# One float32 encoder layer on one core: a recurrence's two score matrices added before their product, the squares of a norm added up on VectorE, two first weight tiles split one block early, and the query and expert blocks made one

## What is computed

```
hn   = modulate(rmsnorm(x), sh1, sc1);  proj = hn @ w_in            # 28 column tiles of 128
o_h  = hgrn2(q, f_fwd, f_bwd, i, g)     # 4 heads: gated linear recurrence in chunks of 64, both ways
         # within a chunk: scores = tril(qr @ kr^T); o_intra = scores @ v   (forward and backward added)
o_c  = silu(layernorm(depthwise_conv31(a * sigmoid(gate))))
h    = x + g1 * (concat(o_h, o_c) @ w_out)                           # 8 column tiles
hn2  = modulate(rmsnorm(h), sh2, sc2)   # mean of squares over the 1024 columns of h
q    = hn2 @ wq                         # 16 tiles: 8 heads x 2 halves; scores against 128 keys each
top16 x top16 -> top16 of 16384 experts per head and token
h    = h + g2 * sum_j softmax_j * gelu(hn2 . u[e_j]) * v[e_j]
out  = modulate(rmsnorm(h), fsh, fsc)
```

## Time and profile before

| what | value |
|---|---|
| median of 3 runs | 2977.69 us (2970.37 to 2980.58) |
| the profiled execution | 2967.23 us, its span 2965.5 us |
| PE busy | 2812.0 us, 95% |
| DVE busy | 2238.2 us, 75% |
| POOL busy | 1257.6 us, 42% |
| ACT busy | 865.6 us, 29% |
| moved by DMA | 911.43 MB, 307 GB/s over the span |

### The profile page before, as it was taken

How to read it: one execution, slowest core, us unless ns; L and a number is a source line. 1 busy time by engine, 2 the same in 40 slices (tenths; PEclk the granted TensorE clock), 3 DMA queues, 4 the chain that set the end, 5 groups by cost and what they waited for, 6 DMA issues and landing times.

```text
span 2965.5 us, 31534 instructions
## 1 busy us (share of the span) xinstructions
PE 2812.0 (95%) x10212; PEld 1534.2 (52%) x10212; DVE 2238.2 (75%) x4571; ACT 865.6 (29%) x1715; POOL 1257.6 (42%) x1091
## 2 busy tenths in 40 slices
PE   6999899897899999999999999999999999999995
PEld 3677677776745444554454545544444444444442
DVE  5898565316789999998998978876767677667675
ACT  3223464213111113673673766810000000000004
POOL 1001110212355445444444454464666566556551
PEclk9999899998899999999999999999999999999998
DMA  4641111232389999999999999999999999999994
GB/s 202 242 177 43 44 36 58 78 116 89 100 342 377 413 374 373 377 377 382 371 373 379 374 376 410 416 408 396 402 404 404 406 392 399 405 406 396 404 388 184
DMA packets 282607, 911.43 MB, mean 307 GB/s; under 512 B 25808, under 2 KB 73168, under 8 KB 275152
## 3 DMA queue, kind: packets, MB, share of 16 engines
q0 software_dynamic: 147456, 536.94, 46.4%
q1 hardware_dynamic: 97648, 297.56, 26.6%
q10 hardware_dynamic: 37344, 74.98, 6.6%
HBM read 826.01 MB, written 83.36 MB: 307 GB/s over the span
## 4 chain that ended last, share of the span: by engine, by line
DVE 20%; DMA 20%; PE 19%; POOL 8%; issue 4%; DVEq 1%; ACT 1%; SPq 1%; another core or an unknown queue 0%; ACTq 0%; POOLq 0%
DMA s_slot<-in_v,s_row 18%; PE s_pu L1711 15%; DVE s_slot L2127 10%; POOL s_slot L1662 8%; PE s_pw L1748 2%; DVE s_hB L2141 2%; PE s_py L1758 1%; DMA s_wr<-s_w 1%; DMA s_slot<-in_u,s_row 1%; DVEq L2162 1%; DVE pk_key L1372 1%; DVE pk_rep L1373 1%; DVE pk_key L1381 1%; DVE s_eq L2036 1%; SPq L1620 0%
## 5 line engine op out<-in xcount | busy, mean ns | idle before, releaser
L1711 PE MATMUL s_pu<-s_hn,s_ut 128*128 128x512 f32 x2304 | 1012.2, 595 | 4.0 <-issue 3.9
L1662 POOL DMA_INDIRECT s_slot<-in_v,s_row x512 | 627.9, 1226 | 385.1 <-DVE s_hB L2141 269.4
L2141 DVE SCALAR_TENSOR_TENSOR s_hB<-s_slot,s_dot,s_hB 128x1024 f32<-128x1024 f32 x469 | 593.9, 1284 | 250.3 <-DMA s_slot<-in_v,s_row 229.2
L1662 POOL DMA_INDIRECT s_slot<-in_u,s_row x512 | 504.9, 986 | 578.1 <-DVE s_slot L2127 492.4
L1711 PEld LDWEIGHTS s_pu<-s_hn,s_ut 128*128 128x128 f32 x2304 | 434.9, 191 | 531.9 <-issue 531.8
L2127 DVE SCALAR_TENSOR_TENSOR s_slot<-s_slot,s_ph 128x1024 f32<-128x1024 f32 x512 | 607.6, 1219 | 65.8 <-DMA s_slot<-in_u,s_row 40.1
L1893 ACT ACTIVATE s_hotw<-s_hot,s_rest 128x128 bf16<-128x128 bf16 x1024 | 308.7, 424 | 27.3 <-ACT s_gst L1840 20.5
L1950 ACT ACTIVATE s_sq<-y 128x512 f32<-128x512 f32 x16 | 8.9, 627 | 921.1 <-DVE y L2202 921.1
L1792 PE MATMUL s_pw<-s_ct,s_vt 128*128 128x512 f32 x512 | 247.5, 606 | 23.5 <-DMA s_vt<-in_v_tiles 23.5
L335 PE MATMUL s_ps<-hn_hi,w_hi 128*128 128x512 f32 x576 | 236.4, 410 | 20.3 <-POOL w_lo L323 11.8
L1792 PE MATMUL s_pu<-s_ct,s_vt 128*128 128x512 f32 x512 | 243.1, 597 | 0.0
(11 more groups left out here) (306 smaller groups left out, 3001.4 us busy)
## 6 DMA issues: line engine op xcount, KB each, us to landing
s_ut<-in_u_tiles SPq DMA_DIRECT2D x128, 512.0 KB
s_vt<-in_v_tiles SPq DMA_DIRECT2D x32, 2048.0 KB
s_g<-s_gst ACTq DMA_DIRECT2D x120, 256.0 KB
s_w<-s_wb ACTq DMA_DIRECT2D x15, 2048.0 KB
s_wr<-s_w SPq DMA_DIRECT2D x16, 1920.0 KB
s_gr<-s_g SPq DMA_DIRECT2D x60, 512.0 KB, 24.8
s_ada<-in_ada SPq DMA_DIRECT2D x48, 512.0 KB, 6.1
s2w_raw<-in_w_in SPq DMA_DIRECT2D x26, 512.0 KB, 3.9
```

Of the source, the lines that this page charges most:

```text
L1662: pool.indirect_dma_start(out=slot[s][:, :], out_offset=None, in_=io[kind], in_offset=bass.IndirectOffsetOnAxis(ap=row[b][:, j:j + 1], axi ...
L1711: mm = pe.matmul(pu[:, n % 2, :], ut[n % UR][:, k, :], hn[:, k, :], start=(k == 0), stop=(k == DC - 1))
L2141: dve.scalar_tensor_tensor(y, s, dot[b][:, j:j + 1], y, ALU.mult, ALU.add).then_inc(taken, 1)
```

## The change

Five edits, and what they move with them:

1. **Scores added first.** After the second part of the state updates DVE adds `st[0]` and `st[1]` into a new tile `st_both`, and PE makes one product of it with the values in place of two.
2. **First tiles split one block early.** At the end of step1 ACT and POOL make both parts of w_in tile 2 (`m.first`), so that ACT's first instruction in `front` is the sigmoid. In `front` they do the same with w_out tile 2 (`m.second`; SP loads it right behind the tiles of `mix`), for step4.
3. **Squares added by DVE.** In step4 DVE adds the squares of columns 0 to 6 (`add_square`) into `sq_sum`; PE makes only two products with ones, at the end.
4. **step5 goes into step6.** All engines have its code unrolled at the head of the expert block, with no barrier between. DVE's constants come ahead of the picks. POOL's two additions for `hn` come behind the remainders of heads 1 and 2. PE's `turn_h` comes behind the last scores, in the order 1, 0, 3, 2, and ACT's softmax behind the copies of them. SP's first u loads wait for the projections that use the same place.
5. **PSUM is shared**: `pu` and `pw` also serve queries and scores, and `ph` and `py` are the accumulators of the blocks before.

```
@@ step1, ACT and POOL, at the end
+            act.wait_ge(ahead, 32)
+            act.activation(m.first[0][:, :, :], m.front_raw[0][:, :, :], ACT.Copy).then_inc(first_hi, 1)
...
+            pool.wait_ge(first_hi, 1)
+            pool.tensor_tensor(m.first[1][:, :, :], m.front_raw[0][:, :, :], m.first[0][:, :, :].bitcast(F32), ALU.subtract)
@@ front
+            sp.dma_start(next_w[0][:, :, :], io["w_out"][2]).then_inc(second_in, 16)
             sp.wait_ge(o_ready, HEADS)
...
-                mm = project(pe, ps[n % 2], w.hi[n % 2], w.lo[n % 2], m.hn_hi, m.hn_lo, ks)
+                hi, lo = m.first if n == 2 else (w.hi[n % 2], w.lo[n % 2])
+                mm = project(pe, ps[n % 2], hi, lo, m.hn_hi, m.hn_lo, ks)
...
-                    pe.matmul(po[:, c], vtok[:, b, :], st[0][:, b, :], start=True, stop=False)
-                    pe.matmul(po[:, c], vtok[:, b, :], st[1][:, b, :], start=False, stop=False)
+                    pe.matmul(po[:, c], vtok[:, b, :], st_both[:, b, :], start=True, stop=False)
...
-            round_tile(2)
             sigmoid(0)
...
             square_of(3)
+            act.wait_ge(second_in, 16)
+            act.activation(m.second[0][:, :, :], next_w[0][:, :, :], ACT.Copy).then_inc(second_hi, 1)
...
                 for part in range(4):
+                    if part == 2:
+                        dve.tensor_tensor(st_both[:, :, :], st[0][:, :, :], st[1][:, :, :], ALU.add)
@@ step4
-            w.round(act, 1, 0)
             w.round(act, 1, 1)
...
-                if k == 2:
-                    sums(0)
-                sums(k - 1)
-            sums(DC - 1)
+            pe.wait_ge(sq_summed, 1)
+            sums(sq_sum, True, False)
+            pe.wait_ge(sq_ready, DC)
+            sums(sq[:, (DC - 1) % 2, :], False, True)
...
+            def add_square(k):
+                dve.wait_ge(sq_ready, k + 1)
...
             for k in range(DC):
+                if k >= 3:
+                    add_square(k - 2)
...
+            add_square(DC - 2)
+            dve.sem_inc(sq_summed, 1)
             dve.wait_ge(root, 1)
@@ step6, POOL
-            for n in range(2):
-                ks = slice(n * DC // 2, (n + 1) * DC // 2)
...
+            for h in range(1, PH):
+                for s in range(2):
+                    wq.remainder(pool, h, s)
+                if h <= 2:
+                    ks = slice((h - 1) * DC // 2, h * DC // 2)
...
@@ step6, PE
-            turn_h(3, pu[:, :, :].rearrange("p a t -> p (a t)"))
-            turn_h(2, pw[:, :, :].rearrange("p a t -> p (a t)"))
...
+            for h in range(1, PH):
+                for s in range(2):
+                    wq.ready(pe, h, s)
+                    pe.wait_ge(q_ready, h * 2 + s + 1)
+                    project(pe, pu[:, s, :], wq.hi[s], wq.lo[s], m.hn_hi, m.hn_lo, halves=(0,)).then_inc(wq.used, 1)
+                    if s:
+                        scores(h, 0)
+                scores(h, 1)
             turn_h(1, py)
             turn_h(0, ph)
+            pe.wait_ge(q_ready, 2 * PH + 2)
+            turn_h(3, pu[:, :, :].rearrange("p a t -> p (a t)"))
+            pe.wait_ge(sc_taken, 2 * PH + 2)
+            turn_h(2, pw[:, :, :].rearrange("p a t -> p (a t)"))
             pe.wait_ge(h_kept, 3)
```

More of the change, by code:

```diff
@@ L156, in step1 @@
         w_in, w_rounded = [sem(f"s1_w_in{s}") for s in range(2)], sem("s1_w_r")
-        ahead = sem("s1_ahead")
+        ahead, first_hi = sem("s1_ahead"), sem("s1_first_hi")
+        m.first = [at(f"s1_first{i}", [P, DC, P], F32R, F0 + (56 + 4 * i) * KB) for i in range(2)]
         m.front_raw = raw_weights(m, "s2w", R0 + 112 * KB)
@@ L491, in _ @@
                 sp.dma_start(next_x[:, i, :], io["xT"][i]).then_inc(next_in, 16)
-                sp.dma_start(next_w[i][:, :, :], io["w_out"][2 + i]).then_inc(next_in, 16)
-            sp.wait_ge(next_in, 64)
+            sp.dma_start(next_w[1][:, :, :], io["w_out"][3]).then_inc(next_in, 16)
+            sp.wait_ge(next_in, 48)
         @block.gpsimd
         def _(pool):
-            for n in range(2, 4):
-                w.remainder(pool, n // 2, n % 2)
+            w.remainder(pool, 1, 1)
             pool.memset(hd.reset[:, :], 1.0)
@@ L1130, in step4 @@
         ps = m.ps
[L1131 removed]
+        m.pu = m.hold.enter_context(nc.psum_tensor("s4_pu", [P, 2, HALF], F32))
+        ps_q = [m.pu[:, s, :] for s in range(2)]
         ps_ss = ctx.enter_context(nc.psum_tensor("s4_ss", [P, T], F32))
@@ L1173, in _ @@
         def _(pool):
-            for k in range(2, DC + 2):
+            for k in range(3, DC + 2):
                 w.remainder(pool, k // 2, k % 2)
@@ L1178, in _, with sums @@
         def _(pe):
-            def sums(k):
-                pe.wait_ge(sq_ready, k + 1)
+            def sums(src, first, last):
                 for h in range(2):
                     mm = pe.matmul(ps_ss[:, h * HALF:(h + 1) * HALF], m.ones[:, :],
-                                   sq[:, k % 2, h * HALF:(h + 1) * HALF], start=(k == 0), stop=(k == DC - 1))
-                mm.then_inc(sq_used, 1)
+                                   src[:, h * HALF:(h + 1) * HALF], start=first, stop=last)
+            pe.sem_inc(w.rounded, 1)
+            pe.sem_inc(w.split, 1)
             w.begin(pe)
@@ L1759, in add_side, with scores @@
                 mm.then_inc(side_done, 1)
-            turn_h(3, pu[:, :, :].rearrange("p a t -> p (a t)"))
-            turn_h(2, pw[:, :, :].rearrange("p a t -> p (a t)"))
+            def scores(h, s):
+                pe.wait_ge(q_ready, h * 2 + s + 3)
+                pe.wait_ge(sc_taken, h * 2 + s + 1)
+                for b in range(SPARSE):
+                    mm = pe.matmul(pw[:, s, b * P:(b + 1) * P], q[s][:, b * P:(b + 1) * P], m.keysT[:, s, :],
+                                   start=True, stop=True)
+                mm.then_inc(sc_made, 1)
+            wq.begin(pe)
+            pe.sem_inc(q_ready, 2)
+            pe.sem_inc(wq.used, 2)
+            for s in range(2):
+                scores(0, s)
+            for h in range(1, PH):
+                for s in range(2):
+                    wq.ready(pe, h, s)
[4 more added lines that the diff above has]
+                scores(h, 1)
             turn_h(1, py)
             turn_h(0, ph)
+            pe.wait_ge(q_ready, 2 * PH + 2)
+            turn_h(3, pu[:, :, :].rearrange("p a t -> p (a t)"))
+            pe.wait_ge(sc_taken, 2 * PH + 2)
+            turn_h(2, pw[:, :, :].rearrange("p a t -> p (a t)"))
             pe.wait_ge(h_kept, 3)
@@ L2217, in _, with encoder_layer @@
                                              ALU.mult).then_inc(xn_ready[h], 1)
-STEPS = (step1, front, step4, step5, step6)
-def encoder_layer(nc, io, out, steps=5, scratch="Internal"):
+    m.hold.close()
+STEPS = (step1, front, step4, step6)
+def encoder_layer(nc, io, out, steps=4, scratch="Internal"):
     m = Mem()
@@ L2268, in sem @@
             return sems[-1]
-        step(nc, m, io if n < 5 else {**io, "out": out}, sem)
+        step(nc, m, io if n < 4 else {**io, "out": out}, sem)
         nc.clear_and_free_semaphores(sems)
```

165 lines of the change are left out of this document (65 added, 100 removed).

## The result

The changed kernel's median is 2956.9 us in 18 runs, that of the kernel before 2977.4 in 18; the ratio is **0.9939, 95% interval 0.9926 to 0.9952**. (It is not the quotient of the two medians, which are 20.5 us apart.) By the ratio that is 18 us (14 to 22) where 25 were forecast: the sign and the range hold, and the size is 7 us short.

What follows compares the result with a forecast made beforehand. PE, busy 95%, was taken as the bound, with DMA also full in the expert block. Terms -1.6 -1 -2.0 -10.5 +6 -16 = -25.1 gave 2942.1 us, scaled to a median of 2952.5; range 2934 to 2969.

Steps and rivals of the forecast that it cites:

- Start of `front`: Start of `front`: PE's gap falls from 5.6 to 4.0 us, the sigmoid being next to be waited for; -1.6.
- Scores added first: Heads 0 to 3: one PE product fewer per 128 tokens, DVE's addition partly unhidden; -1, bounds -7.4 and +3.7.
- Squares on DVE: Step4: turns of 10.9 us in place of 12.64, -10.5; tail +6, as POOL's subtraction delays DVE's last addition.
- rival (c): End of step4: the tail is cheap, clock and port both kind; 4.3 us less, 2948; chance 0.08.
- Seam, PE: Step5 to step6: PE's barrier idle goes, -10.1; faster `turn_h`, -6.5; u passes, -1.5; ACT's last copy, +1.0; together -17.1.
- Seam, DVE and gathers: Step5 to step6: small casts move ahead and the barrier goes; -10.0 for the ranking and first gather.
- I carry -16: Seam term: PE gains 17, gathers 10, DVE makes up the difference from its waits; bounds -10 and -17.6.
- My own sign of being wrong: Expert block: first u tile to last v product stays 2094 us, give or take 3; a longer way means wrong.
- rival (a): Expert block: the gathers set the end, so it gains 10 in place of 16; 2958.5; chance 0.15.
- rival (b): First gathers: the unexplained stall of 9 to 10 us at a u tile goes; -9 more, 2943.5; chance 0.11.
- Rival (d): Expert block: the gain is spent again, PE's v-tile waits grow; -9 left, 2968.6; chance 0.11.
- Rival (e): First gathers: slower, the stall grows with unrolled code and no barrier; five more such tiles give 2996; chance 0.05.

Runs made afterwards that it cites:

- first pair: First profiled execution of each kernel, unedited: 2967.2 us for the kernel before, 2966.4 us for the changed kernel.
- second pair: Each kernel profiled once more, nothing edited: ratio 0.9942 for the changed kernel, 1.000 for the kernel before.
- before, again and paced: Kernel before: unedited (2977.4 us), unedited once more (ratio 1.000), and with POOL's gathers waiting for PE from tile 92 on (0.9981).
- changed, again and paced: Changed kernel: unedited (ratio 0.9939), unedited once more (0.9942), and with POOL's gathers waiting for PE from tile 92 on (0.9896).
- more rows: Changed kernel with row quota 3.7 instead of 3.5 in tiles 30 to 92, 3.8 instead of 4.3 in 93 to 117: ratio 1.0048.
- the wait on POOL's queue: From tile 92 on, rows of tile n+1 are asked for only after PE finishes tile n-2: changed kernel 0.9896, kernel before 0.9981.
- the later tables: Changed kernel with the first turning of picks and the side rows two tiles later: ratio 0.992; with the wait on POOL's queue too, 0.9891.
- the last experiment's: Changed kernel with the two states not added first (two products on PE again, no addition on DVE): ratio 0.9918.

## Why the prediction was right, and where it was off

- **Start of `front`**: -1.6 forecast. The gap fell from 5.60 to 3.47, -2.1, with the sigmoid as the next late thing, as said: the table load moved up too.
- **Scores added first**: -1 forecast, nothing measured. The gap of 2.3 us was right (2.15). What I left out is that a gap of 2.15 us can bring PE out at the lower level of its clock (3.09 us for 16 products in the first profile, 1.71 in the second); in heads 1 to 3 one of 1.1 did not. It is inside the bounds of -7.4 and +3.7.
- **Start of step4**: -2.0 forecast, -1.5 measured.
- **Squares on DVE**: turns of 10.88, six times 1.76 less: -10.6 against -10.5. The tail: +6 forecast, +1.1 measured (from step4's first product to the first of the queries 91.54 us before, 82.04 after, which is -9.5). The step that failed is "so the addition ends at 669.4": DVE's addition followed its residual without a pause, POOL's subtraction began beside it, and POOL's took longer, not DVE's. And the eight passes ran at the upper level, 3.7 us behind a gap of 2.56. That is rival (c), and below my lower bound of +1.7. The lock of the Trainium skill's page "SBUF — State Buffer", "Who interferes with whom", is in the rows, 3.43 us for 2.35, but on POOL; who comes second is the schedule's to say.
- **Seam, PE**: from the last scores to the first u tile 23.9 us before and 8.2 after, -15.7; forecast -10.1, -6.5 and +1.0, together -15.6. `turn_h` took 7.3 us. **Seam, DVE and gathers**: the first gather came 18.9 us earlier, against 9.1 + 10 by the terms (-1.6 -1 -2.0 -4.5 ahead of the seam).
- **First u tile**: -24.5 in all in the first pair, against -24.7 by my terms. That they agree so closely is luck: step4 began at 586.28 before and 586.29 after, so that nothing was left of the 4.6 us forecast ahead of it, and the cheap tail gave 4.9 back. In the second pair step4 began 4.4 us earlier, and the first u tile came 30.5 us earlier.
- **"I carry -16"** is the step that was off. I took PE's gain and let DVE make up the difference. The runs show the other order: at tile 26 PE waits for what follows from the first gather, and tile 28 keeps its 328 to 333 us from that gather. At tile 28 the change leads by 18 us in the mean (before, again and paced, 1156.2; changed, again and paced, 1137.9), and 18 is what was measured. Delays speak for it too, within wide intervals: gathers 14 us later cost 12, PE 28 us later cost 7. My own sign of being wrong came as well: from the first u tile to the last v product it is 2094.0 us before and 2120.3 after, where I wanted 2094 give or take 3. That is rival (a), the gathers, though by a mechanism with a place in it (the wait at tile 26) that the earlier trace rows couldn't show, as PE did not wait there in the profile of before.
- **How much of the 7 us is this step is open.** In the seam term I carried 6 us more than the gathers gained, but the gathers' gain in all, 19 us, also holds the cheap tail. The jam is the other candidate. With it taken from both kernels by the same wait, the change is worth 0.9896 / 0.9981 = 0.9915, 25 us, with some 7 us to either side, which allows both the forecast and the gathers' 19; the wait gave the changed kernel 13 us and the one before 6. The two were timed on different chips, and their profiled executions are 13 us apart.
- **The stall of the earlier trace rows** (rival b) belongs to both kernels, and its size is chance. From the first u tile of the table to ACT's gelu behind tile 0, 16 tiles on, it is 130.4 us in the first profile of the changed kernel, where the stall is absent, and 131.9 with more rows, but 137.1 to 141.6 in the other eight profiles that have the new seam. So rival (b) did not come true as a rule. What the stall takes from PE lies ahead of the wait at tile 26, and the distance from the first gather to tile 28 is the same with it and without it.
- **Rival (d)**, the gain spent again in the expert block, left 9 us; in the first pair of profiles 0.8 are left, and in the medians 18. PE's waits for v tiles, which it expected to grow, are 22.3 us after and 23.5 before. The first profile of before had no jam, that of the changed kernel had.
- **Rival (e)** has its mechanism in the rows, products one by one while gathers have the DMA engines, but not its trigger, unrolled code: the same stood in the kernel before too.
- **The level**: my scaling from one execution to the median assumed a proportion. Most likely the 10 us were one jam that this execution was spared: tiles 96 to 100 took 15 us less than in the second profile.

Best version: the changed kernel with the wait on POOL's queue, 0.9896, or with the later tables too, 0.9891.

## What to carry to other kernels

In a block where DMA is full, measure a lead also at the first transfer of the queue that feeds it, not only at the first product; here an engine's lead over that was mostly slack, and was lost at the next meeting point. A prefetcher that is limited only by its buffers runs ahead when its consumer is free for a while, and fills the DMA engines just when the critical engine should go on: tie it to that engine's progress. A quota did not do it here, a wait did. And take a second profile of the kernel before ahead of any prediction of under 1%: here one 15 us event made two profiles equal that stand for kernels 18 us apart.

## What the runs showed of the hardware

- **While gathers hold the DMA engines, PE, ACT and SP nearly stop together.** For 25 us the gathers had 102.7% of the DMA time and no other queue, an instruction queue included, had a packet; products that were ready came up to 2.1 us apart; three engines went on within 0.05 us. Loads and stores were not kept waiting, as none was left in the queues of SP and ACT. Whether instructions came late isn't shown: in the second profile of before an instruction packet does fall into the like stretch. The Trainium skill, "Runtime: NRT & Kernel Launch", "Instruction fetch mechanics", says that each sequencer fetches code in 16 KiB blocks over a DMA queue of its own, which would fit; "DMA: Bandwidth & Descriptors", "Queues, rings and completion order" in the Trainium skill, says that a DMA engine takes turns between queues that have work, by which a waiting block should get its turn. Both can't explain the rows at once unless nothing was waiting; no run here settles it.
- **The port of DVE and POOL**: with both starting within 0.01 us, behind a DVE instruction, DVE took no longer than alone (1.22 us) and POOL did (3.43 in place of 2.35); in the earlier trace rows, with POOL's start 0.02 us ahead, it was the other way round.
- **The clock**: behind a gap of 2.13 to 2.18 us the 16 products of the fourth part took 1.71 us in 10 of 27 cases and 1.81 to 3.09 in the others (heads 1 to 3 of the nine profiles with the addition); behind one of 1.06 to 1.11, 1.71 in all 15 cases of the five profiles without it. The gap alone does not decide: 16 such products of head 0, behind a gap of 1.07 to 1.08, took 3.05 to 3.61 us in all fourteen profiles; in the last experiment's they took 3.61, at a granted clock of 0.50 from 323.50 to 327.10.
